# Layer 0 of a two-layer backbone: 128 tokens leave the dense value product, and their value rows are gathered by index and summed on VectorE

## What is computed

```python
s1, i1 = lax.top_k(s[..., 0, :], K); s2, i2 = lax.top_k(s[..., 1, :], K)
top_s, top_j = lax.top_k(cand, K)
idx = e1 * N_KEYS + e2                       # 8 heads x 16 = 128 experts a token
gate = jax.nn.softmax(top_s, axis=-1)
...
act = jax.nn.gelu(jnp.einsum('tkd,td->tk', U[it], xt), approximate=False) * gt
return jnp.einsum('tk,tkd->td', act, V[it])
```

## Time and profile before

| what | value |
|---|---|
| median of 3 runs | 3341.94 us (3341.54 to 3345.03) |
| profiled execution, first to last instruction | 3342.5 us |
| TensorE busy | 95% of the span, mean granted clock 0.982 |
| DVE busy | 58% |
| ACT busy | 37% |
| POOL busy | 1% (41 instructions) |
| DMA, mean over the span | 176 GB/s |

### The profile page before, as it was taken

How to read it: one execution, slowest core, us unless ns; L and a number is a source line. 1 busy time by engine, 2 the same in 40 slices (tenths; PEclk the granted TensorE clock), 3 DMA queues, 4 the chain that set the end, 5 groups by cost and what they waited for, 6 DMA issues and landing times.

```text
span 3342.5 us, 48135 instructions
## 1 busy us (share of the span) xinstructions
PE 3169.0 (95%) x19664; PEld 2696.4 (81%) x19664; DVE 1942.5 (58%) x3476; ACT 1222.9 (37%) x1871; POOL 20.0 (1%) x41
## 2 busy tenths in 40 slices
PE   7997889999999999999999998997789999999998
PEld 3664478888888888888888886896689999999998
DVE  5347335998555564444444444436839987656665
ACT  3313233333333333333333334325235444544444
POOL 0000000000000000000000000000000000000000
PEclk9998999999999999999999999998999999999999
DMA  5510223445666556765565552322346777787774
GB/s 204 205 60 1 73 85 98 143 144 153 229 236 221 189 189 199 240 198 195 193 199 193 193 176 70 111 76 92 116 159 200 210 254 256 252 274 260 264 262 165
DMA packets 232610, 587.91 MB, mean 176 GB/s; under 512 B 20983, under 2 KB 104008, under 8 KB 228744
## 3 DMA queue, kind: packets, MB, share of 16 engines
q1 hardware_dynamic: 227280, 528.57, 48.7%
q0 software_dynamic: 4208, 53.27, 4.1%
q10 hardware_dynamic: 904, 3.01, 0.3%
HBM read 483.06 MB, written 101.71 MB: 175 GB/s over the span
## 4 chain that ended last, share of the span: by engine, by line
PE 78%; DVE 14%; ACT 4%; issue 2%; DMA 1%; ACTq 0%; SPq 0%; DVEq 0%
PE ps L555 32%; PE ps L876 26%; PE ps L752 10%; PE ps L828 4%; DVE w_lo L1731 3%; PE ps L788 2%; ACT w_hi L1205 2%; PE ps L635 1%; PE ps L600 1%; DVE arena L1638 1%; DVE arena L1756 1%; DVE arena L1632 1%; PE ps L807 1%; DMA arena<-acts 1%; ACT a_t L1072 1%
## 5 line engine op out<-in xcount | busy, mean ns | idle before, releaser
L1731 DVE TENSOR_TENSOR w_lo<-wring,w_hi 128x1024 fp32r<-128x1024 f32 x512 | 626.4, 1224 | 695.3 <-ACT w_hi L1205 693.1
L555 PE MATMUL ps<-a_hi,w_hi 128*128 128x512 f32 (+1 forms) x2048 | 699.8, 342 | 9.4 <-DVE w_lo L1731 5.5
L876 PE MATMUL ps<-act_hi,w_hi 128*128 128x512 f32 (+1 forms) x2048 | 697.7, 341 | 5.2 <-DVE act_lo L1762 5.2
L555 PE MATMUL ps<-a_hi,w_lo 128*128 128x512 f32 (+1 forms) x2048 | 688.6, 336 | 0.0
L876 PE MATMUL ps<-act_lo,w_hi 128*128 128x512 f32 (+1 forms) x2048 | 688.3, 336 | 0.0
L555 PE MATMUL ps<-a_lo_q,w_hi 128*128 128x512 f32 (+1 forms) x2048 | 688.2, 336 | 0.0
L876 PE MATMUL ps<-act_hi,w_lo 128*128 128x512 f32 (+1 forms) x2048 | 687.8, 336 | 0.0
L1205 ACT CAST w_hi<-wring 128x1024 fp32r<-128x1024 f32 x512 | 533.8, 1043 | 227.7 <-PE ps L876 227.7
L555 PEld LDWEIGHTS ps<-a_hi,w_hi 128*128 128x128 f32 x2048 | 388.3, 190 | 57.0 <-DVE w_lo L1731 8.2
L876 PEld LDWEIGHTS ps<-act_hi,w_hi 128*128 128x128 f32 x2048 | 387.9, 189 | 52.7 <-issue 5.9
L555 PEld LDWEIGHTS ps<-a_hi,w_lo 128*128 128x128 f32 x2048 | 388.4, 190 | 41.0
(11 more groups left out here) (253 smaller groups left out, 3448.5 us busy)
## 6 DMA issues: line engine op xcount, KB each, us to landing
wring<-in_u SPq DMA_DIRECT2D x256, 512.0 KB, 4.0
wring<-in_v SPq DMA_DIRECT2D x256, 512.0 KB, 3.7
gates<-arena POOLq DMA_DIRECT2D x24, 2048.0 KB, 8.6
wring<-in_ada SPq DMA_DIRECT2D x64, 512.0 KB, 5.5
acts<-arena SPq DMA_DIRECT2D x128, 256.0 KB, 4.4
arena<-acts SPq DMA_DIRECT2D x128, 256.0 KB, 3.4
arena<-gates SPq DMA_DIRECT2D x16, 2048.0 KB, 11.2
wring<-in_hgin SPq DMA_DIRECT2D x40, 512.0 KB, 3.4
```

Source lines behind the costliest of these rows:

```text
L555: ins = pe.matmul(o, l, r, start=n == 0, stop=n == len(pairs) - 1, **kw)
L876: ins = pe.matmul(value_sum(l, c), w, x, start=m == 0 and n == 0 and (l == 0 or c % 2 == 0), stop=m == NKEY - 1 and n == 2, skip_group_che ...
L1731: tt(WLO[:, k % 4].rearrange("p k n -> p (k n)"), wring[:, n % RING * TILE:(n % RING + 1) * TILE], WHI[:, k % 4].rearrange("p k n -> p (k ...
```

## The change

`PICK` says how many tokens of a layer leave the dense value product: the first 128 of layer 0, none of layer 1. For these, the 128 experts a token has chosen are handled one rank k at a time, with a token on each of the 128 partitions:

- DVE writes the expert numbers, and the places of the activations in `acts`, into the `hand` tile (`slot_numbers`), once the first tile is routed.
- POOL fetches, by index, 128 rows of V (4 KB for each partition, 512 KB in one transfer, `v_row`) for each k, into a ring of four, and 128 single activations (4 bytes for each partition, `words`) for each k. The activations come in four blocks of 32 transfers; block q+1 stands in POOL's queue ahead of row 32q + 16. A row's fetch waits until the add four rows before is done.
- DVE multiplies 32 activations with their gates once in a block, and adds each row times its activation to a 128x1024 sum (`row_added`). The adds stand behind `low` in the turns 10 to 115 of the V stage.
- TensorE adds that sum, transposed by a matmul with the identity, to the PSUM banks ahead of product 122 (`fold`, 8 matmuls of 128x128).
- The dense part shrinks to 384 tokens in layer 0: 24 matmuls of 128x384 a turn, activations and gates of 384 tokens in loads, DVE and ACT instructions. Gates are made for 48 octs (turns 56 to 103) and stored in 12 groups. The U stage still computes all 512 tokens.

```diff
+PICK = (128, 0)
+DENSE = tuple(w - p for w, p in zip(WIDTH, PICK))
+SPREAD = P // PICK[0]
+QUARTER = PICK[0] // 4
+VRING = 4
+ADD_FIRST = 10
...
 def octs(l):
-    return WIDTH[l] // OCT
+    return DENSE[l] // OCT
...
+def add_turn(k):
+
+    return ADD_FIRST + (NKEY - ADD_FIRST - 12) * k // PICK[0]
+
+
+ADD_TURN = [[k for k in range(PICK[0]) if add_turn(k) == m] for m in range(NKEY)]
+FOLD_TURN = NKEY - 6
...
-                sp.dma_start(ZIN[:, r, 0:WIDTH[l]], acts_out[l][m]).then_inc(z_in[r], 16)
+                sp.dma_start(ZIN[:, r, 0:DENSE[l]], acts_out[l][m, :, PICK[l]:WIDTH[l]]).then_inc(z_in[r], 16)
...
+            def fetch(dst, table, q, k, sem):
+
+                pool.indirect_dma_start(dst, None, table, bass.IndirectOffsetOnAxis(
+                    ap=PSLOT[:, q, k:k + 1].bitcast(U32), axis=0)).then_inc(sem, 16)
+
+            def v_row(k):
+
+                wait(pool, S["row_added"], k - VRING + 1)
+                fetch(VROW[k % VRING], v_rows, 0, k, v_row_in[k % VRING])
+
+            def words(q):
+
+                for k in range(q * QUARTER, (q + 1) * QUARTER):
+                    fetch(PACT[:, k:k + 1], act_cells, 1, k, S[f"act_in{q}"])
+
+            def picked_rows():
+
+                pool.wait_ge(S["part_used"], NKEY)
+                for k in range(2):
+                    v_row(k)
+                for r in range(ZRING):
+                    pool.wait_ge(z_out[r], 16 * (NKEY // ZRING))
+                words(0)
+                for k in range(2, PICK[0]):
+                    if k % QUARTER == QUARTER // 2 and k // QUARTER < 3:
+                        words(k // QUARTER + 1)
+                    v_row(k)
...
-                return ps[:, c, :] if l == 0 else ps[:, 2 + c // 2, c % 2 * SEQ:(c % 2 + 1) * SEQ]
+                return ps[:, c, PICK[0]:T] if l == 0 else ps[:, 2 + c // 2, c % 2 * SEQ:(c % 2 + 1) * SEQ]
+
+            def fold():
+
+                pe.wait_ge(S["fold_ready"], 1)
+                pe.wait_ge(S["row_added"], PICK[0])
+                for c in range(KD):
+                    pe.matmul(ps[:, c, 0:PICK[0]], VACC[:, c * P:(c + 1) * P], FOLD, start=False, stop=True,
+                              skip_group_check=True)
...
                 for m in range(NKEY):
+                    if l == 0 and m == FOLD_TURN:
+                        fold()
...
+            def row_added(k):
+
+                if k % QUARTER == 0:
+                    q = slice(k, k + QUARTER)
+                    dve.wait_ge(S[f"act_in{k // QUARTER}"], 16 * QUARTER)
+                    step.done(tt(PACT[:, q], PACT[:, q], PSLOT[:, 2, q], ALU.mult))
+                dve.wait_ge(v_row_in[k % VRING], 16 * (k // VRING + 1))
+                if k == 0:
+                    ts(VACC, VROW[0], PACT[:, 0:1], None, ALU.mult).then_inc(S["row_added"], 1)
+                else:
+                    dve.wait_ge(S["row_added"], k)
+                    stt(VACC, VROW[k % VRING], PACT[:, k:k + 1], VACC, ALU.mult, ALU.add).then_inc(S["row_added"], 1)
...
                     if m + AHEAD < NKEY:
                         low(l, NKEY + m + AHEAD)
+                    if l == 0:
+                        for k in ADD_TURN[m]:
+                            row_added(k)
```

More of the change, by code:

```diff
@@ L147, in octs, with stored, pool_order @@
 def octs(l):
-    return WIDTH[l] // OCT
+    return DENSE[l] // OCT
 def groups(l):
-    return WIDTH[l] // GTOK
+    return DENSE[l] // GTOK
+def stored(l, b):
+    return sum((groups(x) + 1 - b) // 2 for x in range(l))
+def add_turn(k):
+    return ADD_FIRST + (NKEY - ADD_FIRST - 12) * k // PICK[0]
+ADD_TURN = [[k for k in range(PICK[0]) if add_turn(k) == m] for m in range(NKEY)]
+FOLD_TURN = NKEY - 6
+def pool_order():
+    first = [(oct_turn(0, 4 * g + 3) + OCT_TURNS[0] + 3, 0, g) for g in range(groups(0))]
+    return sorted(first + [(slice_turn(0, 0, SLICES - 1) + 1, 1, 0)])
 EXP_TURN = [{slice_turn(l, i, AT_DIFF) + 2: i for i in range(TILES[l])} for l in range(2)]
@@ L315, in build @@
         I16 = iota[:, 0:TOPK]
+        VROW = [arena[:, at:at + D] for at in range(28672, 28672 + VRING * D, D)]
+        VACC = arena[:, 34560:34560 + D]
+        PSTG = hand[:, 0:3 * P].rearrange("p (q k) -> p q k", q=3)
+        PSLOT = PSTG if SPREAD == 1 else view(33920, "p (q k) -> p q k", q=3, k=PICK[0])
+        PACT = arena[:, 34112:34112 + PICK[0]]
+        FOLD = ident[:, :] if SPREAD == 1 else arena[:, 34240:34240 + PICK[0]]
+        PNUM = hand[:, 3 * P:3 * P + 1]
+        v_rows = a["v0"].rearrange("a b d -> (a b) d")
         def weight_parts(name, hi, lo, ring):
@@ L390, in build @@
         z_in = [sem(f"z_in{r}") for r in range(ZRING)]
+        v_row_in = [sem(f"v_row_in{r}") for r in range(VRING)]
         gates_out = [nc.dram_tensor(f"gates{l}", (groups(l), P, NKEY, GTOK), F32).ap() for l in range(2)]
         acts_out = [nc.dram_tensor(f"acts{l}", (NKEY, P, WIDTH[l]), F32).ap() for l in range(2)]
+        act_cells = acts_out[0].rearrange("a p t -> (a p t)").unsqueeze(1)
         block = ctx.enter_context(nc.Block())
@@ L483, in first_products @@
                         for b in range(2):
-                            sp.wait_ge(S[f"g_stored{b}"], 16 * sum(groups(x) // 2 for x in range(l + 1)))
+                            sp.wait_ge(S[f"g_stored{b}"], 16 * stored(l + 1, b))
                         for x in range(2):
@@ L531, in _, with store @@
             pool.dma_start(arena[:, 8192:10240], a["keys0"]).then_inc(S["keys_in"], 16)
[L534 to L542, removed]
+            def store(l, g):
+                b = g % 2
+                pool.wait_ge(S["g_high"], 2 * l * octs(0) + 8 * (g + 1))
+                pool.dma_start(gates_out[l][g].rearrange("p e t -> p (e t)"), STG[:, b].rearrange("p e t -> p (e t)"))\
+                    .then_inc(S[f"g_stored{b}"], 16)
@@ new lines, in spread_slots @@
+            def spread_slots():
+                n = PICK[0]
+                pool.wait_ge(S["pick_ready"], 1)
+                if SPREAD > 1:
+                    for r in range(SPREAD):
+                        pool.dma_start(PSLOT[r * n:(r + 1) * n], PSTG[0:n, :, r * n:(r + 1) * n]).then_inc(S["pick_in"], 16)
+                    pool.wait_ge(S["pick_in"], 16 * SPREAD)
+            def fetch(dst, table, q, k, sem):
+                pool.indirect_dma_start(dst, None, table, bass.IndirectOffsetOnAxis(
+                    ap=PSLOT[:, q, k:k + 1].bitcast(U32), axis=0)).then_inc(sem, 16)
@@ L543, in _ @@
+            for _, kind, g in pool_order():
+                if kind:
+                    spread_slots()
+                else:
+                    store(0, g)
+            picked_rows()
             pool.wait_ge(S["ck_exp"], 1)
@@ L546, in _ @@
             pool.dma_start(arena[:, 8192:10240], a["keys1"]).then_inc(S["keys_in"], 16)
-            stores(1)
+            for g in range(groups(1)):
+                store(1, g)
         @block.tensor
@@ L1189, in gates_staged @@
                 if n % 4 == 0:
-                    wait(act, S[f"g_stored{g % 2}"], 16 * (l * groups(0) // 2 + g // 2))
+                    wait(act, S[f"g_stored{g % 2}"], 16 * (stored(l, g % 2) + g // 2))
                 for h in range(2):
@@ L1208, in gate_high @@
             def gate_high(l, m):
-                width, r = WIDTH[l], m % ZRING
+                width, r = DENSE[l], m % ZRING
                 act.wait_ge(S["mul_ready"], l * NKEY + m + 1)
@@ L1682, in routing, with slot_numbers @@
                     .then_inc(S["gates_ready"], 1)
+                if l == 0 and i == 0:
+                    slot_numbers()
                 yield
+            def slot_numbers():
+                flat = GATE.rearrange("p q h k -> p q (h k)")
+                dve.wait_ge(S["gates_ready"], 1)
+                dve.tensor_copy(PSTG[:, 2], flat[:, 0])
+                step.done(stt(PSTG[:, 1], flat[:, 1], float(NKEY), flat[:, 2], ALU.mult, ALU.add))
+                dve.tensor_copy(PSTG[:, 0].bitcast(U32), PSTG[:, 1])
+                step.done(ts(PSTG[:, 1], PSTG[:, 1], float(T), PNUM, ALU.mult, ALU.add))
+                dve.tensor_copy(PSTG[:, 1].bitcast(U32), PSTG[:, 1]).then_inc(S["pick_ready"], 1)
             def routes(l):
@@ L1688, in routes, with fold_matrix @@
                         yield
+            def fold_matrix():
+                if SPREAD > 1:
+                    dve.tensor_reduce(FOLD, ident[:, :].rearrange("p (r t) -> p t r", r=SPREAD), AXX, ALU.add)
+                step.done(tt(PSTG[:, 0], ident[:, :], iota[:, :], ALU.mult))
+                dve.tensor_reduce(PNUM, PSTG[:, 0], AXX, ALU.add).then_inc(S["fold_ready"], 1)
+                dve.wait_ge(S["fold_ready"], 1)
+            def row_added(k):
[6 more added lines that the diff above has]
+                    ts(VACC, VROW[0], PACT[:, 0:1], None, ALU.mult).then_inc(S["row_added"], 1)
+                else:
+                    dve.wait_ge(S["row_added"], k)
```

(7 more changed lines are left out.)

9 lines of the change are left out of this document (5 added, 4 removed).

## The result

The changed kernel takes 3316.16 us (median of 4 runs, 3313.21 to 3318.28); the kernel before, on the same chip, 3341.9. The ratio is 0.992, with a 95% interval from 0.9905 to 0.9934. The forecast was 3284 us: the direction came out, but only 25.7 us of the forecast gain of 58.

A forecast was written before the change was run, and what follows sets the result against it. TensorE, busy 95% of the span, was taken as the bound in layer 0. The sum: 3155.0 + 59.4 (adds) - 5 (lead) + 65.4 (blocks) + 2 (fold) + 1.2 (multiplications) + 6.4 (DMA) = 3284.4, forecast 3284 us, range 3220 to 3405.

The forecast's parts named there:

- The blocks: Layer 0's V stage: 32 words queued ahead of rows 16, 48 and 80 stall DVE 21.8 us each, +65.4 us.
- +6.4 for DMA: V stage: a turn's 1551 KB at 325 GB/s takes 4.78 us instead of 4.72, adding 6.4 us.
- the ring alone: V-stage loop gated, gate_high, high, low, next gated through DVE's and ACT's queues; 3.225 us, with one add 4.44, two 5.79.
- What the change removes: U stage: 16 octs fewer, 23.7 us; V stage: 384-column products at 4.16 us, 163.8 us; leaving 3155.0 us.
- What the ring costs with the adds in it: V stage, turns 10 to 115: turns of 4.44 or 5.79 us, +59.4 us, less 5 for a lead at the start.
- What POOL's queue costs: V stage: each later block takes 34 w + 3.7 us against 17.9 us of cover; three stalls, +65.4 us.
- w: Time of one fetch by index on POOL, estimated as 1.06 us, twice the direct form's 0.53.
- The first block: V stage's start: words from about 1360, row 0 wanted at 1402; covered to w = 1.2, beyond that 32 us per us.
- POOL's fetches hold DVE up: Rival, V stage: fetches hold DVE's instructions with two SBUF inputs, 95 us in 106 turns, 3379 us; chance 0.15.
- DMA is the bound: Rival, V stage: DMA engines give only 298 GB/s, +51 us, 3329 us in all; chance 0.07.
- A cheap gather: Rival, POOL's queue: w = 0.53, blocks cost 3.8 us each, 11 in all, 3230 us; chance 0.13.
- a dear gather: Rival, POOL's queue: at w = 2 a block stalls 53.8 us, 3406 us; decides from w = 1.55; chance 0.20.

The follow-up runs named there:

- e1_spread: Against the changed kernel: words of blocks two to four fetched between the rows, nine words for eight rows, from row 2 on; 3223.65 us.
- e4_nogather: Against the changed kernel: POOL's fetches, DVE's adds and the fold left out, so the 128 tokens get no value sum; 3159.14 us.
- e3_addfirst: Against the changed kernel: a turn's adds put ahead of the weights' split `low` instead of behind it, blocks kept; 3273.65 us.
- e2_ring8: Against the changed kernel: eight row buffers in place of four, blocks kept; 3275.73 us.
- the last three runs: e5_both, e6_both_ring8, and e5_both's edits with fetched rows of half the length: 3181.74, 3178.87 and 3172.76 us.
- e5_both: Against the changed kernel: the edits of e1_spread and e3_addfirst together, four row buffers; 3181.74 us.
- e6_both_ring8: Against the changed kernel: the edits of e5_both with eight row buffers in place of four; 3178.87 us.

## Why the prediction was right in its direction and wrong in its size

The runs split the time after into parts, which can be set against the sum. Without gathering: forecast 3155.0, measured 3159.1 (+4.1). All of the gathering except the blocks, which is e1_spread less e4_nogather: forecast 59.4 - 5 + 2 + 1.2 + 6.4 = 64.0, measured 64.5. The blocks: forecast 65.4, measured 92.5 (+27.1). The three differences make 31.7 us, and 3284.4 + 31.7 = 3316.1. That the middle part agrees so well is partly luck: its +6.4 for DMA is not seen in e1_spread, where nearly all turns with one add take 4.41 to 4.48 us and those with two 5.80, as the ring alone has it. What stands in its place is not settled.

**What the change removes** was right. The turns without an oct keep their pace, 42.85 / 189 x 24 = 5.44 us on the chain that ended last, and the first weights' tile of the V stage is issued at 1335.49 where it was 1359.93: 24.4 us, for a forecast of 23.7. Without gathering the V stage takes 534.5 us (e4_nogather, TensorE's products from 1333.67 to 1868.18), for 696.4 - 163.8 = 532.6.

```profile
1289.79 42.85 PE ps L638 x189
```

```profile
1335.49 0.33 SPq L468 DMA_DIRECT2D wring<-in_v  x1
```

Matmuls of 128x384 start 0.173 us apart (five steps from 1440.07 to 1440.93), as the middle of the earlier trace rows had it:

```profile
1440.07 0.33 PE L969 MATMUL ps<-act_lo,w_hi 128*128 128x384 f32 x1
...
1440.93 0.33 PE L969 MATMUL ps<-act_hi,w_hi 128*128 128x384 f32 x1
```

**What the ring costs with the adds in it** was right to a hundredth. `low` starts 1423.36 - 1418.93 = 4.43 us apart with one add and 1429.16 - 1423.36 = 5.80 with two; 4.44 and 5.79 had been worked out from the earlier trace rows. The adds take 1.28 us for an estimate of 1.30:

```profile
L1814 DVE SCALAR_TENSOR_TENSOR arena<-arena x127: 1276/1279/1287, 1383.3 to 1971.6; 128x1024 f32<-128x1024 f32 x127
```

That the cost is the place in the ring and not DVE's time, e3_addfirst shows: the same adds, one line earlier, and the turn is 4.16.

**What POOL's queue costs** is the step that failed: its mechanism and its three places were right, its size was not. The term was 34 w + 3.7 - 17.9 with w = 1.06 for each fetch, twice the direct form's 0.53, which gave 39.7 us from row 15's issue to row 16's landing. Measured in the second block: from 1426.05 to 1475.35, 49.3 us, 9.6 more. Of these, 33 x (1.25 - 1.06) = 6.3 are the undisturbed pace: the fetch itself, 0.94 us, is shorter than its price of 1.06, but the gap of 0.30 us between one fetch and the next had not been counted at all. Another 45.08 - 33 x 1.25 = 3.8 are five fetches that lasted 1.66 to 1.93 us in place of 0.94 while DVE worked. From row 16's issue to its add it was 4.2 us for 4.8 counted, 0.5 less. The cover was 1443.79 - 1426.05 = 17.7 us, for a forecast of 17.9. With w = 45.6 / 34 = 1.34 the same formula gives 31.4 us a block, and the stalls are 31.56 in the second block, 31.7 at the longest, 93.7 in all for the forecast's 65.4. That w lies inside the forecast's own bracket (0.8 to 1.4), but 34 fetches to a block, three times, turn each tenth of a microsecond into 10 us: this was the term to bound most tightly, and it had the least behind it. The price of 1.55 from which the change would not have paid (1.52, if the forecast's own terms are added up again) was 0.2 us away.

**The first block** was covered to w = 1.2 by the forecast; at 45 us for 32 words (1336.11 to 1381.08) DVE waited only 0.59 us. That was luck: DVE stood ready 49 us after the V stage began, not 45, after a wait of 7.07 us for a load of activations at 1342.94. The cover is thin: with the words later or DVE sooner, e2_ring8, e3_addfirst and the last three runs waited 3.7 to 10.0 us.

**POOL's fetches hold DVE up**, the rival: no (its price had DVE 3.3 us a turn in such instructions; by the durations measured it is 3.9). The adds are as long as in the estimate, and `gated` grows from 0.55 to at most 0.605 us. It went the other way. In the second block the fetches of 1.66 us fall in the turns in which DVE worked, and from 1444.91 on, with DVE idle, each lasts 0.94 or 0.95. The summary of all fetches (minimum, median, maximum in ns):

```profile
L593 POOL DMA_INDIRECT arena<-in_v,hand x128: 933/1010/1935, 1332.9 to 1956.3; - x128
L593 POOL DMA_INDIRECT arena<-acts,hand x128: 940/944/1975, 1336.1 to 1782.2; - x128
```

Where the two overlap, the trace shows that DVE's instruction is what a fetch waits for, and not the load on the DMA engines. The 22 fetches of the V stage that start while a `low` runs last 1.17 to 1.98 us, and each ends 0.80 to 0.83 us after that `low` does: above, the fetch of 1429.54 ends at 1431.21, and the `low` of 1429.16 at 1430.38. The 129 that start beside no DVE instruction last 0.93 to 0.99. The other way round nothing is held: the 99 `gate_low` that start inside a running fetch last 0.54 to 0.56 us, as the others do.

The Trainium skill (SBUF — State Buffer, section "Who interferes with whom") has VectorE's instructions with two SBUF inputs and GpSimd's reads of SBUF contend, and leaves it to the order of issue who waits. The trace agrees where DVE was first: POOL then waited up to about 1 us a fetch. That DVE waits where the fetch was first it does not show; DVE's instructions grew by some 0.05 us at most.

**DMA is the bound**, the rival: not in the changed kernel, where the stage's mean share is 0.77 and the loads of activations cost one wait of 7.1 us, at the stage's start; e4_nogather has one of 5.5 in the same place. **A cheap gather** and **a dear gather** both fall with the measured w.

The version that beats both kernels is e5_both, 4.8% under the kernel before and 4.1% under the changed one (3181.74 / 3316.16 = 0.959; these two were not measured side by side). e6_both_ring8 can't be told from it.

## What to carry to other kernels

Price a queue from start to start, gap included and beside a busy neighbour, and multiply before trusting it: a small error in one fetch is 34 times as large in a block of them. A block of cheap requests ahead of an urgent one in a queue that works in order costs the block's whole length less what the consumer has in store; spreading the requests took the stalls away here, as long as the queue still had room between the urgent ones, and a deeper ring buys at most its own depth. Work added to an engine with idle time is free only where it doesn't stand between two steps of a ring: look for the wait in that engine's own queue and put the work ahead of it.

## What had not been expected of the hardware

- A fetch by index costs POOL the same for 128 words of 4 bytes as for 128 rows of 4 KB or 2 KB: the shortest are 0.940, 0.933 and 0.940 us, with 0.30 us to the next.
- The granted clock falls to 0.50, the lower level of 1.2 GHz, in the gap of the second block, with TensorE idle. After it twelve matmuls started 0.32 us apart in place of 0.173 (1477.72 to 1481.38), some 1.8 us. It cost nothing here: the turn with two adds behind it, at DVE, was 5.81 us against 5.80 elsewhere.
- One core's DMA engines moved 368 to 370 GB/s for long stretches at a share of 1.01, with rows fetched by index among the loads, and TensorE was busy 98 to 100% there.
